# First choice of experts without tile 1's products between its steps, and the first group's mixing bias added by VectorE

## What is computed

```
va_n = layernorm(gelu(va)) * ln_v_g + ln_v_b
z[t] = sum_{s<=t} w_s[g][t,s] * va_n[s] + b_s[g][t]      # per channel group g (8 x 128), chunks of 128 positions
y_a  = gelu(ua) * z
m    = sigmoid(g_a) * (y_a @ w_br_a) + sigmoid(g_b) * (y_b @ w_br_b)
x1   = layernorm(alpha * x + m @ w_o)
q    = x1 @ w_q          # 8 heads, two halves of 128 each, normalised
s    = q . keys          # 128 scores per half; top 16 of each, top 16 of the 256 sums -> 16 experts and gates
y[t] = sum over heads and experts of gate * gelu(x1[t] . u_tab[e]) * v_tab[e]
x2   = layernorm(alpha * x1 + y);  x3 = x2 + (p @ w_pe) * sigmoid(x2 @ w_pg)
```

## Time and profile before

| | |
|---|---|
| median of three runs | 1952.78 us (1948.48 to 1953.85) |
| profiled execution | 1945.02 us |
| its span | 1943.3 us, granted clock 0.837 in the mean |
| busy in the span | TensorE 1425.5 us, VectorE 1166.8, GpSimd 988.5, ScalarE 402.3 |
| read from HBM | 667.07 MB |
| DMA engines' share, gathers | 71.4% |
| DMA engines' share, plain transfers | 17.4% |

### The profile page before, as it was taken

How to read it: one execution, slowest core, us unless ns; L and a number is a source line. 1 busy time by engine, 2 the same in 40 slices (tenths; PEclk the granted TensorE clock), 3 DMA queues, 4 the chain that set the end, 5 groups by cost and what they waited for, 6 DMA issues and landing times.

```text
span 1943.3 us, 19827 instructions
## 1 busy us (share of the span) xinstructions
PE 1425.5 (73%) x6736; PEld 894.8 (46%) x6736; DVE 1166.8 (60%) x2987; ACT 402.3 (21%) x819; POOL 988.5 (51%) x1052
## 2 busy tenths in 40 slices
PE   8999998798977879989894995354733346674565
PEld 7888887675553456556561553022401011230113
DVE  1110113887677566676678765877878867866511
ACT  2320201242341221232111221111321211211010
POOL 0000000446664546565565765776767776767761
PEclk9999999898997889998997998777866655687778
DMA  7336541799999999999999999999999999999993
GB/s 275 128 133 237 193 155 40 263 386 384 408 411 372 394 384 408 412 411 411 409 403 399 392 410 412 410 408 400 407 370 409 404 407 364 404 374 407 408 381 126
DMA packets 172597, 675.82 MB, mean 348 GB/s; under 512 B 19497, under 2 KB 22697, under 8 KB 158674
## 3 DMA queue, kind: packets, MB, share of 16 engines
q0 software_dynamic: 149760, 545.33, 71.4%
q1 hardware_dynamic: 22738, 129.23, 17.4%
HBM read 667.07 MB, written 7.41 MB: 347 GB/s over the span
## 4 chain that ended last, share of the span: by engine, by line
PE 38%; DMA 28%; DVE 17%; POOL 9%; issue 6%; ACT 1%; SPq 0%; DVEq 0%; POOLq 0%; PEldq 0%; ACTq 0%
DMA at<-in_v_tab,idxV 16%; PE PJ L1445 14%; DMA at<-in_u_tab,idx 8%; PE Y L1495 7%; DVE at L1215 6%; POOL at L679 5%; PE PJ L1343 5%; PE PJ L1327 4%; POOL at L670 4%; PE PJ L1350 3%; DMA at<-in_state 2%; PE PJ L1404 1%; DMA out_st_s<-at 1%; DVE at L1143 1%; DVE at L1081 1%
## 5 line engine op out<-in xcount | busy, mean ns | idle before, releaser
L670 POOL DMA_INDIRECT at<-in_u_tab,idx x512 | 487.9, 953 | 610.7 <-DVEq L1198 342.2
L1215 DVE CUSTOM_DVE_ANT_0 at<-at,XD 128x1024 f32<-128x1024 f32 x512 | 616.0, 1216 | 232.0 <-DMA at<-in_u_tab,idx 220.2
L1495 PE MATMUL Y<-at,at 128*32 128x512 f32 x2048 | 357.9, 824 | 394.8 <-DMA at<-in_v_tab,idxV 394.8
L679 POOL DMA_INDIRECT at<-in_v_tab,idxV x512 | 483.9, 945 | 298.2 <-PE Y L1495 167.5
L1445 PE MATMUL PJ<-at,at 128*128 128x256 f32 (+1 forms) x1792 | 414.1, 391 | 4.4 <-issue 1.7
L1445 PEld LDWEIGHTS PJ<-at,at 128*128 128x128 f32 x1792 | 343.2, 194 | 77.8 <-issue 20.5
L1495 PEld LDWEIGHTS Y<-at,at 128*32 128x32 f32 x2048 | 74.8, 134 | 591.0 <-issue 589.0
L1343 PE MATMUL PJ<-at,at 128*128 128x256 f32 (+2 forms) x960 | 224.1, 393 | 6.2 <-DVE at L1122 5.4
L1343 PEld LDWEIGHTS PJ<-at,at 128*128 128x128 f32 (+2 forms) x960 | 170.1, 180 | 62.8 <-issue 14.3
L1327 PE MATMUL PJ<-at,at 128*128 128x256 f32 (+1 forms) x640 | 143.5, 383 | 0.0
L1327 PEld LDWEIGHTS PJ<-at,at 128*128 128x128 f32 (+1 forms) x640 | 108.7, 171 | 40.6 <-issue 14.3
(11 more groups left out here) (208 smaller groups left out, 1271.6 us busy)
## 6 DMA issues: line engine op xcount, KB each, us to landing
at<-in_w_blk SPq DMA_DIRECT2D x72, 1024.0 KB, 7.4
at<-in_w_q SPq DMA_DIRECT2D x16, 1024.0 KB, 8.0
at<-in_w_o SPq DMA_DIRECT2D x8, 1024.0 KB, 7.1
at<-in_u_tab,idx POOLq DMA_INDIRECT x512, 11.4
at<-in_v_tab,idxV POOLq DMA_INDIRECT x512, 11.3
at<-in_state SPq DMA_DIRECT2D x4, 1024.0 KB, 8.4
out_st_s<-at SPq DMA_DIRECT2D x4, 1024.0 KB, 6.6
at<-in_w_pg SPq DMA_DIRECT2D x2, 2048.0 KB, 13.6
```

Source lines behind the costliest of these rows:

```text
L670: pool.indirect_dma_start(ubuf[slot], None, u_tab, bass.IndirectOffsetOnAxis(rows_of, 0)).then_inc(u_in[slot], 16)
L679: pool.indirect_dma_start(vbuf[slot], None, v_tab, bass.IndirectOffsetOnAxis(rows_of, 0)).then_inc(v_in[slot], 16)
L1215: v.tensor_tensor_reduce(out=t, in0=t, in1=XD[:, :], scale=1.0, scalar=0.0, op0=ALU.mult, op1=ALU.add, accum_out=hraw[:, n % 2, k:k + 1]). ...
L1495: last = mm(Y[32 * c:32 * c + 32, s, :], wpadV[d // PAIR % 2][:, g, :], vbuf[slot][:, 512 * s:512 * s + 512], start=False, stop=final)
```

## The change

It does two things. The bias of group 0's mixing jobs is no longer a product: it is loaded once more, spread over all 128 partitions (`z_bias`, in Q[1], which is not in use until the queries of tile 1), and VectorE adds it to the sum in PSUM before it multiplies. Group 1 keeps the one-row products. In the list, the first choice runs to its end without products of tile 1 between its steps; these three follow it, among the parts of the second choice; tile 1's normalisation moves to slots 6 and 8 of step -1, and its turning from behind wq[3] to behind wq[7].

```
@@ plan() @@
-    out += wo[1][1:2] + second[:2] + first[4:5] + second[2:3] + wo[1][2:3] + first[5:6] + wo[1][3:] + first[6:]
-    out += second[3:4] + wq[2:3] + second[4:5] + x1[1] + second[5:6]
+    out += second[:2] + first[4:5] + second[2:3] + first[5:] + wo[1][1:2] + second[3:4] + wo[1][2:3] + second[4:5]
+    out += wo[1][3:] + wq[2:3] + second[5:6]
...
-    behind = spread_over(wq[3:4] + turn(0, "t1", 1) + wq[4:] + mixers(1) + close + wq2[:1], (-1, 0), (13, 6))
+    behind = spread_over(wq[3:PH] + turn(0, "t1", 1) + wq[PH:] + mixers(1) + close + wq2[:1], (-1, 0), (13, 6))
...
+    for part, e in enumerate(x1[1]):
+        behind[-1, 6 + 2 * part] = [e] + behind.get((-1, 6 + 2 * part), [])
@@ decoder_step @@
+        z_bias = Q[1].rearrange("p a b -> p (a b)")[:, 0:G * 128].rearrange("p (a b) -> p a b", a=G)
...
+            sp.dma_start(z_bias, b_s.rearrange("a (b c) -> (a b) c", b=G).partition_broadcast(128)).then_inc(zb_in, 16)
@@ VectorE, z @@
-                    v.tensor_tensor(t, t, src[:, 0:4 * p].rearrange("p (a b) -> p a b", a=4), ALU.mult).then_inc(pj_dve, 1)
+                    z = src[:, 0:4 * p].rearrange("p (a b) -> p a b", a=4)
+                    if g == 0:
+                        z_b = z_bias[:, 4 * i:4 * i + 4, :]
+                        v.wait_ge(zb_in, 16)
+                        link(v.tensor_tensor(z, z, z_b, ALU.add))
+                    v.tensor_tensor(t, t, z, ALU.mult).then_inc(pj_dve, 1)
@@ TensorE, z @@
-                        mm(out[:, a * p:(a + 1) * p], values(c)[0:p, k * 128:(k + 1) * 128], w, start=True, stop=False)
-                        last = mm(out[:, a * p:(a + 1) * p], ones[0:1, :], b, start=False, stop=True)
+                        last = mm(out[:, a * p:(a + 1) * p], values(c)[0:p, k * 128:(k + 1) * 128], w, start=True, stop=g == 0)
+                        if g:
+                            last = mm(out[:, a * p:(a + 1) * p], ones[0:1, :], b, start=False, stop=True)
```

More of the change, by code:

```diff
@@ L498, in decoder_step @@
         x_in = [sem(f"x_in{i}") for i in range(KC // 2)]
-        x2_in, gl_in, small_in, row_in, ws_in = (sem(n) for n in ("x2_in", "gl_in", "small_in", "row_in", "ws_in"))
+        x2_in, gl_in, small_in, row_in, ws_in, zb_in = (sem(n) for n in ("x2_in", "gl_in", "small_in", "row_in", "ws_in", "zb_in"))
         blk_in = [sem(f"blk_in{i}") for i in range(RING)]
```

## The result

| | before | changed |
|---|---|---|
| median, four runs each | 1951.24 us (1948.48 to 1953.85) | **1932.69 us** (1930.78 to 1935.64) |
| ratio | | **0.9915**, 95% interval 0.9903 to 0.9928 |
| profiled execution, its span | 1945.02 us, 1943.3 | 1935.64 us, 1933.9 |

By the ratio the changed kernel is faster by 16.6 us (14 to 19); the two medians lie 18.55 us apart. That is more than the 0.3% that a measurement can tell, and more than was forecast: 1942 us, range 1935 to 1951. The two profiled executions lie only 9.4 us apart, since that of before was 6 us under its own median and that of after 3 us over.

What follows compares the result with a forecast made beforehand. TensorE was taken to bound the first stage and the gathers the long one, so an earlier start comes off the end. 5.9 + 4.7 = 10.6 us off the median of 1952.78 gave 1942 us, range 1935 to 1951.

Steps and rivals of the forecast that it cites:

- the stages: Whole kernel: a first stage bound by TensorE, a handover working out the first choice, a long one bound by gathers.
- the waits: VectorE ahead of the third choice's scores: a wait of 6 to 9 us instead of 4.03.
- the lead at the third choice: Third choice's scores: 4.7 us earlier by part two, 10.6 us with both parts, and handed on to the end.
- Part one: Group 0's mixing jobs: bias products leave TensorE, VectorE adds instead; 5.9 us earlier, bounds 5.1 and 6.2.
- The new load: 512 KB more on SyncE's queue in the first ten microseconds: taken as 0, 1.4 us without cover.
- Part two: First choice without tile 1's products: first gather 9.4 us earlier, third choice's scores 4.7 us, bounds 0.7 and 7.3.
- one fall of the clock: TensorE after its pause ahead of tile 1's turning: half clock once, costing about 2.6 us on this path.
- The first rival: TensorE's clock stays up behind the first turning and at wq(0,1): gain 16.3 us, 1936 us; chance 0.12.
- The second: Part two handed back by a clock fall in both products or late rows for first dots: 1946 us; chance 0.20.
- the third: Long stage starts from the second group's weight loads, which take up the gain: at most 3 us, 1950 us; chance 0.11.
- the fourth: Slower: v gathers' waits of 167.5 us grow; 6.3% eats the gain, 12% gives 1962 us; chance 0.07.
- The fifth: ScalarE's order still keeps VectorE between the first choice's steps: 5.9 and perhaps 3 us; counted within the second.

Runs made afterwards that it cites:

- early_third: The changed kernel with tile 1's normalisation and turning put behind the third choice's products; 1928.77 us, ratio 0.9891 to the kernel before.
- order_only: The kernel before with only the new order of the list, its one-row bias products kept; ratio 0.9947, in repeats 0.9992 and 0.9978.
- norm_ahead: The changed kernel with tile 1's normalisation ahead of the first dots and its turning where the kernel before had it; ratio 0.9923.
- bias_full_height: The order of before, with group 0's bias products kept but made 128 rows high; a single execution took 1939.41 us beside before's median of 1948.71.
- before_2: The kernel before, unaltered, as a control on another chip; ratio 0.9967 (0.9921 to 1.0013).

## Why the prediction was wrong

The sign, the stages and the waits were right. So was, for this change, that the lead at the third choice is handed on; early_third shows that it isn't always. The size was not: 10.6 us forecast, 16.6 measured, and the time fell out of the range on the low side. What was missing is a cost in the kernel before, the change of height.

**Part one is the step that failed.** The sum had 16 x 0.415 - 0.7 = 5.9 us, with bounds of 5.1 and 6.2; the branch product came 8.9 us earlier in the mean (262.6 to 253.7). The term mis-sized is the price of what is taken away. The 0.83 us between two bias pairs were halved, as if the full pair beside each were at its natural pace. It wasn't: alone it takes 0.22 us. From the first mixing product to the branch product 34.82 us became 26.02: 8.8 us, and 9.5 without the 0.7 for the last addition, where the sum had 6.6. The 8.9 of the means are these 8.8, 0.7 more for the fall of the clock in two of before's five profiles, and 0.6 less because the mixing jobs happen to start later in the changed kernel's five (227.7 us against 227.1). The price of the natural pace stood in the profile before, as products of 256 columns at 7.07 us for 32, 0.22 us a row or 0.11 for 128 columns, and I didn't set the pair's 0.2075 a row beside it. The bounds were put around the small added operation (0.4 to 1.5 us, measured 0.70) and none around the large removed one. The new load cost nothing that shows: the mixing jobs start at 227.4 us in the mean of the ten profiles that have it, and at 227.4 in that of the eight of before and order_only.

**Part two was sized right.** From the first top-16 to the first gather it took 325.75 - 315.20 = 10.55 us, forecast 10.6. The first gather came 18.8 us earlier in the first profile: 7.9 of the branch product, 1.4 of faster products behind the first turning, 9.5 of part two (forecast 9.4). The first dot came 22.8 us earlier; less the same 9.3, 13.5 are left, as forecast. The third choice's first top-16 came 13.75 earlier, 4.5 of them by part two (forecast 4.7 of 0.7 to 7.3). In order_only it stands 115.6 us behind the branch product, in before 120.6: 5.0. VectorE waited 8.69 us there (forecast 6 to 9). The pause ahead of the turning (5.14 us) and one fall of the clock, in the turning and wq(0,1) and not in wq(1,1), were as forecast. Here the rule of the Trainium skill that was weighed (TensorE: Matmul & The Clock Gate, "What's actually happening") is borne out by the long pause, 1.94 us for the turning and 6.65 for 16 rows. But the fall behind the first mixing job, in four profiles, has no pause ahead of it. norm_ahead shows that without the long pause the path is only 0.6 to 0.8 us shorter.

**The first rival came true in part.** The products behind the first turning took 8.4 us in the mean instead of 9.7, 1.2 us more gain. Whether this belongs to the change is not settled: the same 32 products took 8.55 to 10.14 us in five executions of before, 7.14 to 8.83 in five of the changed kernel, and 7.14 and 10.14 in two of early_third, which is the same up to there; bias_full_height, with the order of before, has 7.14. **The second** (handed back) fell with the third choice's time, **the third** (nothing shows) with gather 49, **the fourth** with the waits of the v gathers, 170.0 us after 167.5: 1.5% instead of the 6.3% at which it would decide. **The fifth** fell with VectorE's rows.

**From lead to time.** With the right price the sum is 8.9 + 1.2 + 4.9 = 15.0 us, the mean lead at the third choice, which would have given 1938 us from the median of 1952.78 that I started from. That median came out at 1951.24 with one more run, and the rest, 3.6 us, is within what the ratio leaves open (14 to 19 us). So the range was too narrow for two reasons: no bound above 6.2 for part one, and no room for the spread of the runs themselves, which is 5 us from the lowest to the highest of three.

## What to carry to other kernels

When small operations are woven into large ones, price their removal by the pitch of the pattern against the pitch of the large ones alone, and look whether their weight loads still run ahead. A step that stands between two stages is worth what it moves at the first event behind which nothing differs any more (here gather 49, not the scores ahead of it), and that event, read from means where there were several profiles, agreed with the gain of five kernels within their intervals. When one wait is taken away, look which engine is waited for next: in early_third the v buffers gave back 6 of 14 us. Products of another tile don't belong in an in-order queue between the steps that the next stage waits for: three additions of 0.4 us each, with the waits for their products, put the first gather off by 9.5 us.

## What the hardware showed beside that

**Height.** One-row and 128-row float32 products of 128 columns in turn go at 0.2075 us a row, 128-row ones alone at 0.11, and a one-row product of 512 columns with its way back costs 1.05 us for two rows.

**Adding in PSUM.** A VectorE addition of 128x512 float32 from PSUM and SBUF into PSUM takes 0.70 us, the multiplication of the same size out of PSUM 0.69.

**Chips.** The same kernel took 1951 us in the first comparison, 1949 in one group and 2050 to 2055 in four. Up to gather 49 little differs (459.4 us in before's first profile, and 461.0 to 464.9; in the changed kernel 447.2, and 445.2 to 447.7); the long stage does. Stretch from 1000 to 1500 us, columns as in the earlier trace rows, of before in its first profile and of before_2:

```profile
1000.00:1500.00 500.00, 294.85 (x1493) 149.60 (x1491) 379.48 (x994) 104.22 (x212) 334.02 (x353) 0.78 1.01 402
```

```profile
1000.00:1500.00 500.00, 292.06 (x1459) 156.80 (x1457) 337.31 (x883) 94.49 (x194) 303.25 (x319) 0.76 0.95 370
```

There 370 GB/s come in instead of 402, and VectorE does 883 operations instead of 994. The granted clock is nearly the same. What limits those chips wasn't tried.
